# Two layers of a hybrid decoder: the retention state's outer product between the tiles of the next group, auxiliary steps one per group, gating behind the weight remainder

## The reference, cut to what matters

```python
def token_mixing(xn, pos, mem_k, mem_v, s_ret, s_gdn, conv_buf, p):
    r_q, r_k, r_v, r_g, g_qkv, g_z, g_a, g_b, m_q, gates = jnp.split(xn @ p['w_in'], W_IN_SPLITS, axis=-1)
    o_ret, s_ret = retention_branch(r_q, r_k, r_v, r_g, pos, s_ret)
    o_gdn, s_gdn, conv_buf = gated_delta_branch(g_qkv, g_z, g_a, g_b, conv_buf, ...)
    o_mem = memory_attention(m_q, mem_k, mem_v)
    merged = (gate[:, :, 0] * (o_ret @ p['w_branch_ret'])
              + gate[:, :, 1] * (o_gdn @ p['w_branch_gdn'])
              + gate[:, :, 2] * (o_mem @ p['w_branch_mem']))
    return merged @ p['w_out'], s_ret, s_gdn, conv_buf
```

## Time and profile before

| what | value |
|---|---|
| median of 3 runs | 2229.37 us |
| the profiled execution, its own time | 2230.65 us |
| its span, first to last instruction | 2229.1 us |
| TensorE busy | 2006.3 us (90%) |
| VectorE, ScalarE, GpSimd busy | 61%, 39%, 5% |
| mean granted TensorE clock | 0.943 |
| mean transfer rate | 165 GB/s |

### The profile page before, as it was taken

The page is one execution under the profiler, slowest core; times in us unless marked ns, Lnnn a source line. Parts: engine busy times, 40 slices in busy tenths (PEclk is TensorE's granted clock), DMA queues, the critical chain, the costliest instruction groups (busy, mean ns, idle before and its releaser), DMA issues.

```text
span 2229.1 us, 42021 instructions
## 1 busy us (share of the span) xinstructions
PE 2006.3 (90%) x15506; PEld 1952.3 (88%) x15506; DVE 1368.5 (61%) x2021; ACT 880.2 (39%) x941; POOL 112.2 (5%) x173
## 2 busy tenths in 40 slices
PE   4999999898989999599979998999988899959996
PEld 4999988898888999599979998889978899958996
DVE  4655566755547667655566557575643767775555
ACT  3443435234342244344344434442443323434433
POOL 1000000010100000000000000010111001000000
PEclk8999999898999999699999999998999889979998
DMA  6665646554533455465656655574545335544654
GB/s 207 187 181 162 185 152 208 175 189 153 189 127 122 154 162 175 138 184 164 180 153 188 170 172 169 166 235 154 178 151 187 117 99 185 165 116 141 179 167 136
DMA packets 435711, 368.81 MB, mean 165 GB/s; under 512 B 9394, under 2 KB 413236, under 8 KB 435442
## 3 DMA queue, kind: packets, MB, share of 16 engines
q1 hardware_dynamic: 411440, 278.76, 42.0%
q0 software_dynamic: 24112, 87.98, 12.2%
HBM read 341.06 MB, written 25.64 MB: 165 GB/s over the span
## 4 chain that ended last, share of the span: by engine, by line
PE 64%; DVE 19%; issue 9%; ACT 5%; DMA 2%; DVEq 1%; SPq 0%; ACTq 0%; POOLq 0%
PE proj L594 15%; PE proj L595 14%; PE proj L596 14%; PE proj L614 3%; PE proj L616 3%; PE proj L615 3%; DVE wl L1504 2%; PE aux L769 2%; ACT wh L1126 2%; PE aux L634 1%; DVE sring L1876 1%; DVE y L1638 1%; DVE junk L1712 1%; DVE c_t L1953 1%; DVE t_t L2041 1%
## 5 line engine op out<-in xcount | busy, mean ns | idle before, releaser
L594 PE MATMUL proj<-xh,wh 128*128 128x264 f32 x2688 | 815.4, 303 | 57.9 <-DVE wl L1504 31.0
L595 PE MATMUL proj<-xl,wh 128*128 128x264 f32 x2688 | 780.0, 290 | 0.0
L596 PE MATMUL proj<-xh,wl 128*128 128x264 f32 x2688 | 778.3, 290 | 0.0
L1504 DVE TENSOR_TENSOR wl<-raw,wh 128x2048 fp32r<-128x2048 f32 (+1 forms) x282 | 603.7, 2141 | 188.6 <-ACT wh L1126 160.3
L1126 ACT CAST wh<-raw 128x2048 fp32r<-128x2048 f32 (+1 forms) x282 | 504.7, 1790 | 469.2 <-PE proj L596 340.2
L594 PEld LDWEIGHTS proj<-xh,wh 128*128 128x128 f32 x2688 | 527.1, 196 | 69.9 <-issue 62.9
L595 PEld LDWEIGHTS proj<-xl,wh 128*128 128x128 f32 x2688 | 526.6, 196 | 1.0
L596 PEld LDWEIGHTS proj<-xh,wl 128*128 128x128 f32 x2688 | 522.7, 194 | 0.0
L614 PE MATMUL proj<-hh,wh 128*128 128x264 f32 x704 | 202.4, 288 | 3.3 <-DVE wl L1504 2.9
L616 PE MATMUL proj<-hh,wl 128*128 128x264 f32 x704 | 199.7, 284 | 0.0
L615 PE MATMUL proj<-hl,wh 128*128 128x264 f32 x704 | 199.7, 284 | 0.0
(11 more groups left out here) (388 smaller groups left out, 2830.7 us busy)
## 6 DMA issues: line engine op xcount, KB each, us to landing
raw<-ffn_w_in SPq DMA_DIRECT2D x176, 512.0 KB, 4.9
raw<-w_in SPq DMA_DIRECT2D x80, 1024.0 KB, 6.1
raw<-ffn_w_out SPq DMA_DIRECT2D x64, 704.0 KB, 4.7
sring<-cache_mem_k POOLq DMA_DIRECT2D x32, 512.0 KB, 4.9
sring<-cache_mem_v POOLq DMA_DIRECT2D x32, 512.0 KB, 3.9
out<-sring POOLq DMA_DIRECT2D x32, 512.0 KB, 3.5
sring<-state_gdn POOLq DMA_DIRECT2D x32, 512.0 KB, 5.2
raw<-w_mem_v SPq DMA_DIRECT2D x10, 1024.0 KB, 6.1
```

The lines of the kernel that those rows point to most:

```text
L594: pe.matmul(o, a, c, start=(k == 0), stop=False)
L595: pe.matmul(o, a, d, start=False, stop=False)
L596: mm = pe.matmul(o, b_, c, start=False, stop=(k == KT - 1))
L1504: dve.tensor_sub(wl[:, slot, 0:size], raw[:, slot, 0:size], wh[:, slot, 0:size].bitcast(F32)).then_inc(split_done[slot], 1)
```

## The change

The step list, TensorE's hooks, ScalarE's and VectorE's parts of x2 and rg are changed; nothing is computed differently.

- The outer product of sequence g-1 and VectorE's update of its state move from behind group g-1 to between the tiles of group g; the last (rS7) stands behind group 7, after the other steps.
- The other steps of x2 are one per group: gcol and gev (0), gct0 (1), gct1 and gn0 (2), gn1 (3), gn2 (4), gn3 (5), gvn0 (6), gqd and gvn1 (7). gkn moves between the tiles of rg's group 0. `STEPS` follows, and so do the banks.
- ScalarE copies gev raw in group 0, ahead of the silu, and does its exponential in place in group 1; it takes the logarithms one per group, and the two copies to `vn` from VectorE (new milestone gvnd).
- In VectorE's `merge_tile` of x2 the hook between the tiles is called in even groups too. In rg `stream` has a new hook `late`, behind the split, that does the product of rout with r4 and the gated tiles.

```diff
-         + [x for g, more in enumerate((("gcol", "gev"), ("gct0", "gct1"), ("gn0", "gn1"), ("gn2", "gn3"), ("gvn0",), ("gvn1",),
-                                        ("gkn",), ("gqd",))) for x in (f"rd{g}", f"rS{g}") + more]
-         + ["gd0", "rn0", ...
+         + [x for g, more in enumerate((("gcol", "gev"), ("gct0",), ("gct1", "gn0"), ("gn1",), ("gn2",), ("gn3",), ("gvn0",),
+                                        ("gqd", "gvn1", "rS7")))
+            for x in ((f"rS{g - 1}",) if g else ()) + (f"rd{g}",) + more]
+         + ["gkn", "gd0", "rn0", ...
@@ TensorE
+                def update_retention(g):
+                    if g:
+                        outer(f"rS{g - 1}", kdb, g - 1, g)
                 def prepare_delta(g):
-                    outer(f"rS{g}", kdb, g, g + 1)
                     if g == 0:
...
-                    elif g == 1:
-                        ready("tail")
-                        for z in range(2):
-                            turn(l, f"gct{z}", [(j * P, tail[:, 8 * z + j, :]) for j in range(8)])
-                    elif g in (2, 3):
-                        ready("gsq")
-                        square_sums(2 * g - 4)
-                        square_sums(2 * g - 3)
...
+                    if g in (1, 2):
+                        if g == 1:
+                            ready("tail")
+                        turn(l, f"gct{g - 1}", [(j * P, tail[:, 8 * g - 8 + j, :]) for j in range(8)])
+                    if g in (2, 3, 4, 5):
+                        if g == 2:
+                            ready("gsq")
+                        square_sums(g - 2)
+                    if g == 7:
+                        ready("gprod")
...
+                    if g in (6, 7):
+                        turn(l, f"gvn{g - 6}", [(j * P, qkvt[:, 8 + j, (g - 6) * P:(g - 5) * P]) for j in range(KT)])
+                    if g == 7:
+                        update_retention(8)
-                products(l, "x2", ..., after=prepare_delta, inner=read_retention)
+                products(l, "x2", ..., after=prepare_delta, mid=update_retention, inner=read_retention)
+                def turn_keys(g):
+                    if g == 0:
+                        ready("gqk")
+                        turn(l, "gkn", ...)
+                products(l, "rg", xh, xl, after=finish_retention, mid=turn_keys, inner=read_delta)
@@ ScalarE
                 def prepare_delta(g):
                     if g == 0:
+                        order(act.copy(egb[:], take(act, l, "gev")[:, 0, 0:2 * H * NS]))
+                        release(act, "gev")
                         ready("conv_p")
                         order(act.activation(qkvt[:, :, 0:SEQ], qkvt[:, :, 0:SEQ], ACT.Silu))
                     elif g == 1:
...
-                        o = take(act, l, "gev")
-                        order.apart(act.activation(egb[:, 0:H * NS], o[:, 0, 0:H * NS], ACT.Exp))
-                        order(act.copy(egb[:, H * NS:], o[:, 0, H * NS:2 * H * NS]))
-                        release(act, "gev")
+                        order(act.activation(egb[:, 0:H * NS], egb[:, 0:H * NS], ACT.Exp))
...
+                    elif g < 6:
+                        j = g - 2
+                        o = take(act, l, f"gn{j}")
+                        order(act.activation(sqg[:, 2 * j:2 * j + 2, :], o[:, :, 0:T], ACT.Ln, bias=epst[:]))
+                        release(act, f"gn{j}")
+                        if g == 5:
                             order(act.activation(sqg[:], sqg[:], ACT.Exp, scale=-0.5))
                             tell("gqr")
+                    else:
+                        order(act.copy(vn[:, g - 6, :], take(act, l, f"gvn{g - 6}")[:].rearrange("p a b -> p (a b)")))
+                        release(act, f"gvn{g - 6}")
...
@@ VectorE
                     size, _ = two_on(name, ph, i, u)
                     split(l, u % 2, use(l, ph, i, u) + 1, size)
+                    if late:
+                        late(4 * i + u)
@@ merge_tile
                     if u % 2 == 0:
+                        if mid:
+                            mid(4 * i + u)
                         return
@@
+                def update_retention(g):
+                    if g:
+                        unit_wait(dve, l, R_UNIT + g - 1)
+                        update(f"rS{g - 1}", (R_UNIT + g - 1) % SRING, lambda h: decay[h])
                     if g + 1 < NS:
                         one_row(kdb, g + 1)
+                def prepare_delta(g):
                     order(cp(rds[:, :, g], take(dve, l, f"rd{g}")[:, 0, 0:KT]))
                     release(dve, f"rd{g}")
-                    unit_wait(dve, l, R_UNIT + g)
-                    update(f"rS{g}", (R_UNIT + g) % SRING, lambda h: decay[h])
...
+                    elif g < 3:
+                        z = g - 1
+                        order(cp(cso[:, z * 1024:(z + 1) * 1024], flat(f"gct{z}")[0:27, :]))
+                        release(dve, f"gct{z}")
...
                     elif g == 7:
                         for h in range(H):
                             c = slice(2 * h, 2 * h + 2)
                             order.apart(stt(rout[:, c, SEQ:T], rds[:, c, :], decay[h], rsv[:, c, :], ALU.mult, ALU.add))
                         order.wait()
                         tell("rof")
+                        order(cp(qkb[:], take(dve, l, "gqd")[:, 0, 0:H * NS]))
+                        release(dve, "gqd")
+                        update_retention(8)
-                stream(l, "x2", merge_tile(l, True), after=prepare_delta)
+                stream(l, "x2", merge_tile(l, True, update_retention), after=prepare_delta)
@@ rg
                 def finish_retention(g):
+                    if g == 0:
+                        order(cp(kn[:].rearrange("p n d -> p (n d)"), flat("gkn")))
+                        release(dve, "gkn")
                     read_delta(g)
...
+                def gate_retention(g):
+                    if g == 1:
+                        ready("rlr")
+                        order(tt(rout[:]..., r4[:]..., ALU.mult))
+                    elif g == 2:
+                        gated((0, 1, 2, 3))
+                    elif g == 3:
                         gated((4, 5, 6, 7))
                         tell("o_ret")
-                stream(l, "rg", after=finish_retention)
+                stream(l, "rg", after=finish_retention, late=gate_retention)
```

More of the change, by code:

```diff
@@ L113 @@
               "conv_s gsq gqr gqk tail cso bcd gexp geb dm dme g_at "
-              "gvb gvn0d gsg gvb1 gvn1d gqd gS_out gof g2sq glr o_gdn ").split()
+              "gvb gvnd gvn0d gsg gvb1 gvn1d gqd gS_out gof g2sq glr o_gdn ").split()
 def build(nc, x_prompt, x_sample, mem_prompt, state_ret, state_gdn, state_conv, cache_mem_k, cache_mem_v,
@@ L945, in decays @@
                         end(mm, f"{step}{s}")
+                def turn_keys(g):
+                    if g == 0:
+                        ready("gqk")
+                        turn(l, "gkn", [((2 * h + t) * P, qkvt[:, 4 + h, t * P:(t + 1) * P]) for h in range(H) for t in range(2)])
                 def finish_retention(g):
@@ L1380, in prepare_delta @@
                         tell("gexp")
[L1381 to L1386, removed]
+                    elif g < 6:
[4 more added lines that the diff above has]
+                        if g == 5:
                             order(act.activation(sqg[:], sqg[:], ACT.Exp, scale=-0.5))
                             tell("gqr")
+                    else:
+                        order(act.copy(vn[:, g - 6, :], take(act, l, f"gvn{g - 6}")[:].rearrange("p a b -> p (a b)")))
+                        release(act, f"gvn{g - 6}")
+                        if g == 7:
+                            tell("gvnd")
                 stream(l, "x2", through(l, ACT.Sigmoid, "gate"), after=prepare_delta)
@@ L1504, in split, with stream @@
                 dve.tensor_sub(wl[:, slot, 0:size], raw[:, slot, 0:size], wh[:, slot, 0:size].bitcast(F32)).then_inc(split_done[slot], 1)
-            def stream(l, name, tile=None, after=None, groups=None):
+            def stream(l, name, tile=None, after=None, groups=None, late=None):
                 def body(ph, i, u):
@@ L1906, in prepare_delta @@
                         tell("bcd")
[L1907 to L1918, removed]
+                    elif g < 3:
+                        z = g - 1
+                        order(cp(cso[:, z * 1024:(z + 1) * 1024], flat(f"gct{z}")[0:27, :]))
+                        release(dve, f"gct{z}")
+                        if g == 2:
+                            tell("cso")
+                            ready("gexp")
+                            order(ts_(ex[:, 8:16], ex[:, 8:16], -1.0, None, ALU.mult))
+                            ready("geb")
+                    elif g == 6:
                         ready("gqr")
@@ L1924, in prepare_delta @@
                         tell("gprod")
-                    elif g == 5:
-                        order(cp(vn[:, 1, :], flat("gvn1")))
```

(10 more changed lines are left out.)

13 lines of the change are left out of this document (3 added, 10 removed).

## The result

The changed kernel takes 2196.3 us (median of 4 runs, 2192.48 to 2200.28) against 2228.99 before (4 runs): ratio 0.9838, interval 0.9804 to 0.9872. Forecast were 2203.6 in a range of 2191 to 2217. It is faster by 1.6%, inside the range, and by more than the likeliest case: 32.7 us where 27.0 were worked out.

What follows compares the result with a forecast made beforehand. The prediction took TensorE as the bound, through its idle time and its time at the lower clock. x2's 30.4 us less 3.4 for clock dips, with rg 0, gave 27.0: 2230.65 - 27.0 = 2203.6 us, range 2191 to 2217.

Steps and rivals of the forecast that it cites:

- The waits of x2: From group 1's end to rn0 in x2: 70.3 us per layer against 85.5, gaining 15.2 per layer, 30.4 in both.
- The new waits: TensorE's waits in the new order of x2: 1.6 us ahead of gn0, 1.1 ahead of rS7, 0.2 for rd5.
- The contents: TensorE's work from x2's group 1 end to rn0, counted at full clock: 67.4 us per layer.
- The clock: One dip of TensorE's clock per layer, for the gn0 wait in x2: 3.4 us given back, bounds 0 and 6.8.
- The table loads: Two more ScalarE table loads per layer in x2, 1.28 us each, hidden except where a bank is released; no drain counted.
- rg gives 0: Moving rg's gated tiles behind the split reorders VectorE's work but removes nothing: gain 0, bounds 0.28 x 2 to 11.4 us.
- new wait ahead of gy00: At x0's first gy step, TensorE would wait 4.8 us for t_m once the wait ahead of x0 is gone.
- VectorE's unbroken row: In rg and the start of x0, VectorE works from 655.36 to 681.92 with gaps of 0.4 us at most.
- TensorE as the limit of rg: Rival: the 5.69 us wait ahead of x0 is gained in full in both layers; 2192 us, chance 0.10.
- Half of x2 coming back: Rival: three x2 waits (gn0, rS7, rd5) grow by about 1 us, with clock dips; 2216 us, chance 0.17.
- ScalarE never held a bank: Rival: in x2, rd5, rS5 and rd7 wait for ScalarE in mid-group; slower, 2253 us, chance 0.03.
- The time freed in x2: Rival: x2's gain is waited for again behind it, as VectorE bounds layer by layer; 2229 us, chance 0.04.

Runs made afterwards that it cites:

- e8: The changed kernel with VectorE's copy of gct1 to cso done twice, lengthening the wait ahead of gn0; 2198.82 us (2 runs).
- e5: The changed kernel with rd2 in bank 1, so gct1 and gn0 share no bank, and the copy of qkb first; 2192.73 us.
- e9: The changed kernel with the changes of e5 and e7, and rout's product with r4 moved from VectorE to GpSimd; 2186.55 us (6 runs).
- e10: The changed kernel with the changes of e5 and e7 together, without GpSimd's part; 2190.36 us (6 runs).
- e1: The changed kernel with rg's gating ahead of the split again, x2 as changed; 2197.78 us (4 runs).
- e2: The kernel before with only rg's gating moved behind the split; 2231.9 us (10 runs), ratio 1.0004.
- e6: The padded kernel: the changed kernel with eight extra copies on VectorE in rg that nobody reads; 2216.68 us (3 runs).
- e7: The changed kernel with the two copies to t_m moved from VectorE to ScalarE; 2190.51 us (4 runs).
- e4: The kernel before with only the outer products and state updates moved between the tiles; 2206.91 us, ratio 0.9903.
- e3: The kernel before with only gev copied by ScalarE ahead of the silu, its exponential done in place later; 2216.8 us, ratio 0.9947.

## Why the prediction was right, and where its sizes were off

- **The waits of x2.** Forecast 70.3 us from group 1's end to rn0, measured 69.49 in both layers; so 16.0 and 16.1 us gained where 15.2 stood in the sum. The new waits were 1.45 and 0.96 (forecast 1.6 and 1.1; the terms given for the second, 2.2 less 1.0, make 1.2), and between rS4 and gn3 the tiles' stretch is at most 0.2 longer than its neighbours. The contents were some 0.5 too dear.
- **The clock.** This is the term of the sum that was mis-sized. I gave back 3.4 us, 1.7 per layer, for a dip behind gn0; the granted clock there was 1.00, and e8 had none behind 2.70 us either. The 6.5 us that the clock gave back within x2 were in the sum all the same, since the new contents were counted at full clock. The nearest rows were no rule: the second and third row had already given two answers for one wait.
- **What the clock gave on top.** Not in my sum: behind rn0 the changed kernel has no dip where the kernel before had one in both layers (1.7 and 1.6 us), and group 1 of layer 1 spends less time at the lower clock (1.6 us: 1605.30 to 1619.44 were 14.1 at a granted clock of 0.76, now 1589.56 to 1602.06 are 12.5 at 0.86, as in layer 0). I had left group 1 as it was. The first of these, 3.3 us, is in part luck, since e5, e8, e9 and e10 have the dip behind rn0 again in one layer or both. The second stands in all ten traces of kernels with a changed x2. Without the 4.9 us the time would still lie inside the range.
- **The sum.** Layer 0: 0.1 in group 1, 16.0, 1.7, less 0.3 from gbr0 to gkS, 17.5. Layer 1: 1.6 + 16.1 + 1.6 - 0.3 = 19.1. Together 36.6, less than the 38.2 between the two profiled executions' spans and more than the 32.7 between the medians. The rest lies outside the changed stages. The changed kernel's four runs stand in two pairs, 2192.48 and 2192.76, 2199.83 and 2200.28; I have no trace of the upper pair.
- **The table loads.** The forecast left out any drain behind them. The changed kernel has two loads more per layer, and no wait of 1.4 us ahead of rd5, rS5 or rd7 shows up. Around the load at 545.16 the cast ahead ends at 545.14 and the logarithm begins at 546.46, 0.02 behind the load's end. The trace so disagrees with the 1380 ns of drain per switch that the Trainium skill gives (ScalarE: Activation LUTs, "What ACT_TABLE_LOAD costs"), as far as a cost in this chain goes.
- **rg gives 0.** Shown by e1 and e2 from both sides, and its reason by e6 and e7. Forecast were 4.8 us of new wait ahead of gy00, measured 4.34, and 47.2 us from VectorE's copy of gd1 to gkS, measured 47.5 (619.05 to 666.55). What the forecast called VectorE's unbroken row begins behind the second wait for ScalarE; the distance holds both of these waits, which the forecast didn't name.
- **The rivals.** TensorE as the limit of rg is refuted by e2. Half of x2 coming back did not happen: the waits did not grow, and no dip stood behind them. ScalarE never held a bank for more than 0.2 us in mid-group. The time freed in x2 did pass through: VectorE still idles 11.22 us ahead of rg's block.

## What to carry to other kernels

A step that writes a buffer and the step that next needs that buffer should have a stretch of other work between them as long as the reader's update. When steps move, walk through the buffers' rotation in the new order: the early release of gev's bank alone left two thirds of x2's gain behind, the new place of the outer product alone more than a third. The largest wait of a stretch is not its price: before moving work to remove it, follow the engine that ended it to its next idle time. If it has none before TensorE needs it again, a new order only moves the wait. Then work has to come off that engine or, which was not tried here, go into a wait that the engine itself has further up.

## What was not expected of the hardware

Dips of TensorE's clock came and went without a change of the work around them. With the same wait of 2.5 to 2.6 us ahead of the second rn sum, rn0 to gbr0 takes 15.8 us in the changed kernel, e1, e4, e6 and e7, 17.3 to 17.5 in e2, e8 and e10, and one of each, layer by layer, in e3, e5 and e9. A dip costs 1.6 to 1.7 us each time. In the padded kernel the clock was 0.53 over 30.7 us in gq, with TensorE busy for 28.63 of them, and the execution took some 15 us more ahead of the edit. Differences of 3 to 8 us between kernels here are better read from distances in the traces than from times.
